# Convolution loop of a decoder step: the splitting of weight units 4 to 15 moves from GpSimd to ScalarE and VectorE

## The chip, the core and the metric

The kernel runs on one core of one Trainium2 chip. The metric is the device time of one execution in microseconds (us), and a profile of one execution shows what each engine did: TensorE (PE, with its weight loads as PEld), VectorE (DVE), ScalarE (ACT), GpSimd (POOL) and the queue of SyncE (SP), which issues loads.

## The reference

A step of a small decoder trunk: layer 0 is a Conformer convolution module with a SwiGLU feed-forward, layer 1 stick-breaking attention with another. There are 1024 prompt positions and 8 x 4 sample positions, 1056 columns in all, with 1024 channels in float32. The change lies in the first half of the convolution module:

```python
def conformer_conv(h, buf, w_pw1, b_pw1, w_dw, b_dw, ln_g, ln_b, w_pw2, b_pw2):
    a = h @ w_pw1 + b_pw1
    d = a.shape[-1] // 2
    u = a[..., :d] * jax.nn.sigmoid(a[..., d:])
    full = jnp.concatenate([buf.astype(u.dtype), u], axis=1)
    new_buf = full[:, full.shape[1] - (CONV_WIDTH - 1):]
    c = lax.conv_general_dilated(
        full, w_dw[:, None, :].astype(u.dtype), window_strides=(1,), padding='VALID',
        dimension_numbers=('NWC', 'WIO', 'NWC'), feature_group_count=d) + b_dw
    c = jax.nn.silu(layer_norm(c, ln_g, ln_b))
    return c @ w_pw2 + b_pw2, new_buf
```

`h` is the RMS-normed input, `w_pw1` is 1024 x 2048, and the depthwise convolution has 31 taps for each channel.

## The kernel before, in words

**Weights in two halves.** A product keeps float32 precision with operands of the rounded type fp32r: each weight w is split into wh, its rounding, and wl = w - wh, and each activation into xh and xl. `project` (L1255) multiplies wh by xh, wh by xl and wl by xh for each of 8 blocks of 128 input channels, so 24 matmuls of 352 columns for a tile. The weights come as a stream of units of 128 x 1024 (128 output channels, 512 KB). SP loads unit u into `w_raw` (2 slots) once unit u - 2 is split, GpSimd rounds it into `wh` (CAST, L530) and subtracts to make `wl` (TENSOR_TENSOR, L532), rings of 4 slots each. A slot may be written when the unit four before it is used up, which TensorE says with `w_done` at the first matmul of its next unit. `w_split` counts finished low halves, `w_hi` the roundings, `w_in` the loads. `unit_ready(u)` on TensorE waits until unit u has both halves.

**Chunks.** The convolution works on 8 chunks of 128 channels. Chunk c uses units 2c (linear half) and 2c+1 (gate half). On TensorE a chunk is: wait for both units; for each of three column tiles, project the linear half into a bank A and the gate half into a bank B (144 matmuls in all, L1255); then the last seven of the 31 taps as matmuls with diagonal matrices (28 matmuls, L1302; chunk 6 has 8 taps and chunk 7 has 16 there); they wait for the gated rows. Then comes the next chunk.

**ScalarE**, for chunk c (`conv_chunk`): builds the diagonals (L680) once the taps of chunk c - 1 are done, takes the sigmoid of each gate tile (L686), issues the store of u_tail, and after the taps of chunk c copies their sums with the bias into `cv` (L694), where VectorE adds the rest.

**VectorE** makes the gated rows of a chunk (`glu_rows`, L976, L982: three tiles into `ub` or, for odd chunks, into the memory of `ssq`) and then the other 24 taps (`conv`, L1000, 48 operations of 128x512, for two column halves; 46 and 30 in chunks 6 and 7). It is written one chunk behind: rows of chunk c+1, then taps of chunk c. The loop on VectorE:

```python
        glu_rows(0, 0)
        with v.Fori(0, KC // 2 - 1) as it:
            glu_rows(it, 1)
            conv(it, 0)
            glu_rows(it + 1, 0)
            conv(it, 1)
        glu_rows(KC // 2 - 1, 1)
```

**GpSimd** splits units 0 to 15 in a loop (`split_units(0, UNITS_CONV)`), then computes the convolution of the sample positions for chunks 0 to 5 and then for 6 and 7 (`decode_conv`, L558 and L561, 62 operations for each part; the first part waits for the rows of chunk 5, the second for those of chunk 7), and then goes on with units 16 and up. Behind the taps come the layer norm's mean (L1316), variance (L1324) and the second projection.

Of the kernel before, what the change touches and what calls it, by code (L numbers as in the profile page):

```python
# [20 lines left out]
F32 = mybir.dt.float32  # L21
F32R = mybir.dt.float32r
I32 = mybir.dt.int32
ALU = mybir.AluOpType
ACT = mybir.ActivationFunctionType
# [4 lines left out]
KC = D // P  # L30
# [14 lines left out]
LOOP_CHUNKS = KC - 2  # L45
# [3 lines left out]
def pe_taps(c):  # L49
    return LATE_PE_TAPS[c - LOOP_CHUNKS] if isinstance(c, int) and c >= LOOP_CHUNKS else PE_TAPS  # L50


def conv_ops_before(c):

    late = range(LOOP_CHUNKS, c) if isinstance(c, int) else ()
    return c * CONV_OPS - 2 * sum(pe_taps(i) - PE_TAPS for i in late)
SLOT = PAD + NQ
RMS_EPS, LN_EPS = 1e-6, 1e-5
RAW, RING = 2, 4
# [25 lines left out]
UNITS_CONV = U_PW2  # L85
# [68 lines left out]
def wait_alone(eng, semaphore, value):  # L154

    eng.wait_ge(semaphore, value)
    eng.sem_inc(PASSED[0], 1)
# [11 lines left out]
def build(nc, x_t, params, wstream, conv_state, cache_kt, cache_v, page_table, bias_row, bias_dec,  # L169
# [3 lines left out]
    def sem(name):  # L173
        return ctx.enter_context(nc.semaphore(name))

    def sb(name, shape, dt=F32, stack=None):
        return (stack or ctx).enter_context(nc.sbuf_tensor(name, shape, dt))
# [7 lines left out]
    w_raw = sb("w_raw", [P, RAW, KC * P])  # L185
    wh = sb("wh", [P, RING, KC * P], F32R)
    wl = sb("wl", [P, RING, KC * P], F32R)
# [71 lines left out]
    def diag(k):  # L259
        return diag_memory[k // 8][:, k % 8 * P:(k % 8 + 1) * P]  # L260
# [11 lines left out]
    def pcol(name, c):  # L272
        if isinstance(c, int):
            return par[:, off[name] + c:off[name] + c + 1]
        return par[:, ds(c + off[name], 1)]
# [4 lines left out]

    w_in = [sem(f"w_in{i}") for i in range(RAW)]
    w_hi = sem("w_hi")
    w_split = sem("w_split")
    w_done = sem("w_done")
    x_in = [sem(f"x_in{tg}") for tg in range(NTG)]
# [26 lines left out]
    class Glu:  # L312
# [6 lines left out]
        conv = sem("conv_step")  # L319
# [10 lines left out]
        act = sem("ln_act")  # L330
# [168 lines left out]
    def _(pool):  # L499
# [22 lines left out]
        def split_units(first, last):  # L522
            with pool.Fori(0, (last - first) // 4) as it:
                for s in range(4):
                    u = it * 4 + (first + s)
                    q, r = divmod(first + s, RAW)
                    pool.wait_ge(w_in[r], (it * (4 // RAW) + (q + 1)) * 16)
                    wait_alone(pool, w_done, u + 2)
                    slot = (first + s) % RING
                    pool.tensor_copy(wh[:, slot], w_raw[:, r]).then_inc(w_hi, 1)  # L530
                    pool.wait_ge(w_hi, u + 1)
                    pool.tensor_tensor(wl[:, slot], w_raw[:, r], wh[:, slot].bitcast(F32), ALU.subtract)\  # L532
                        .then_inc(w_split, 1)

        split_units(0, UNITS_CONV)


        pool.wait_ge(us_in, 16)
# [87 lines left out]
    def _(act):  # L626
# [45 lines left out]

        act.wait_ge(par_in, 16)
        act.wait_ge(n_mix0.ready, NTG * KC)
        def conv_chunk(it, u):
            c = it * 2 + u
            taps = pe_taps(c)
            wait_alone(act, Glu.taps, c + 1)
            for k in range(taps):
                mm = act.activation(diag(k), ident[:], ACT.Copy, scale=pcol("w_dw", c * W + (W - taps + k)))  # L680
            mm.then_inc(Glu.diag, 1)
            for tg in range(NTG):
                j = it * (2 * NTG) + (u * NTG + tg)
                act.wait_ge(Glu.done, j + 1)
                wait_alone(act, Glu.out, j + 3)
                act.activation(sq[:, tg % 2], B[tg][:, 0:TG], ACT.Sigmoid, bias=pcol("b_pw1", c + KC))\  # L686
                   .then_inc(Glu.sig, 1)

            wait_alone(act, Glu.out, it * (2 * NTG) + (u * NTG + 3 + NTG))
            act.dma_start(u_tail[ds(c, 1)].rearrange("a p n -> (a p) n"), ubs[u][:, SEQ:SEQ + PAD])\  # L690
               .then_inc(Glu.saved[u], 16)
            wait_alone(act, Glu.taps, c + 2)
            for h in range(2):
                ins = act.activation(cv[:, ds(c, 1), h * QT:(h + 1) * QT].rearrange("p a t -> p (a t)"), DN[h][:],  # L694
                                     ACT.Identity, bias=pcol("b_dw", c))
            ins.then_inc(Glu.init, 1)

        with act.Fori(0, LOOP_CHUNKS // 2) as it:
            conv_chunk(it, 0)
            conv_chunk(it, 1)  # L700
        conv_chunk(LOOP_CHUNKS // 2, 0)
        conv_chunk(LOOP_CHUNKS // 2, 1)
        act.dma_start(us_tail, us[:]).then_inc(Glu.dec_saved, 16)


# [213 lines left out]
    def _(v):  # L919
# [47 lines left out]
        def glu_rows(half, u):  # L967

            c = half * 2 + u
            for tg in range(NTG):  # L970
                v.wait_ge(Glu.sig, c * NTG + (tg + 1))
                if tg == 0:
                    v.wait_ge(Glu.saved[u], half * 16 + 16)
                    v.wait_ge(Glu.conv, c * CONV_OPS + CONV_OPS)
                n = TG if tg < NTG - 1 else PT2
                ins = v.scalar_tensor_tensor(out=ubs[u][:, PAD + tg * TG:PAD + tg * TG + n], in0=A[tg][:, 0:n],  # L976
                                             scalar=pcol("b_pw1", c), in1=sq[:, tg % 2, 0:n],
                                             op0=ALU.add, op1=ALU.mult)
                if tg == NTG - 1:
                    row = us[:, c, :, PAD:SLOT] if isinstance(c, int) else \  # L980
                        us[:, ds(c, 1), :, PAD:SLOT].rearrange("p a b q -> p (a b) q")
                    ins = v.scalar_tensor_tensor(  # L982
                        out=row, in0=A[tg][:, PT2:TG].rearrange("p (b q) -> p b q", q=NQ), scalar=pcol("b_pw1", c),
                        in1=sq[:, tg % 2, PT2:TG].rearrange("p (b q) -> p b q", q=NQ), op0=ALU.add, op1=ALU.mult)
                ins.then_inc(Glu.out, 1)

        def conv(half, u):

            c = half * 2 + u
            v.wait_ge(Glu.init, c + 1)  # L990
            done = conv_ops_before(c) + 2 * CONV_OPS
            for k in range(W - pe_taps(c)):
                tap = par[:, off["w_dw"] + c * W + k:off["w_dw"] + c * W + k + 1] if isinstance(c, int) else \
                    par[:, ds(c * W + (off["w_dw"] + k), 1)]
                for h in range(2):
                    out = cv[:, c, h * QT:(h + 1) * QT] if isinstance(c, int) else \
                        cv[:, ds(c, 1), h * QT:(h + 1) * QT].rearrange("p a t -> p (a t)")
                    if k:
                        v.wait_ge(Glu.conv, done + (2 * k + h - 1))
                    v.scalar_tensor_tensor(out=out, in0=ubs[u][:, h * QT + k:h * QT + k + QT], scalar=tap, in1=out,  # L1000
                                           op0=ALU.mult, op1=ALU.add).then_inc(Glu.conv, 1)


        glu_rows(0, 0)
# [3 lines that stand above are left out]
            glu_rows(it + 1, 0)  # L1008
            conv(it, 1)
        glu_rows(KC // 2 - 1, 1)  # L1010
        conv(KC // 2 - 1, 0)
        conv(KC // 2 - 1, 1)


        def ln_centre(tg):
# [632 lines left out]
```

## Time and profile before

| | |
|---|---|
| median of 3 runs | 2946.99 us (2940.54 to 2951.22) |
| profiled execution, its own time | 2943.93 us |
| its span, first to last instruction | 2941.9 us |
| busy: PE, PEld | 2753.4 us (94%), 2619.8 us (89%) |
| busy: DVE, ACT, POOL | 1295.7 us (44%), 646.2 us (22%), 1063.8 us (36%) |
| mean granted clock of TensorE | 0.962 of full speed |

Shares of the whole span say little here, since the stages differ: the projection and feed-forward stages fill TensorE, while in the convolution loop, from about 60 to 412 us, VectorE is busy most of the time. Times in the rows are microseconds from the start of the span. Operations on one engine overlap a little, so a group's time divided by its count is nearer to the spacing of two operations than the duration of one is.

### The profile page before, as it was taken

Reading aid. Unit: us, or ns where it says so; the run is one execution under the profiler, and the core shown is the slowest. Engines: PE = TensorE matmul, PEld = TensorE weight load, DVE = VectorE, ACT = ScalarE, POOL = GpSimd, SP = SyncE. Lnnn points to the kernel's source line nnn. Section 1 sums busy time; section 2 is a strip of 40 time slices with the busy share of each in tenths; the row PEclk is TensorE's granted clock in tenths of the full one; section 3 lists DMA queues with packets and bytes.
Section 4 is the critical chain, followed back from the end, with each engine's and each line's share of the span. In section 5 each row is a group of like instructions: output and inputs, shape, how many; then the busy total and the mean of one; then the engine's idle time right before and its main releaser. Section 6 shows DMA issues by size and latency. Waiting matters only on the chain.

```text
span 2941.9 us, 42757 instructions
## 1 busy us (share of the span) xinstructions
PE 2753.4 (94%) x16800; PEld 2619.8 (89%) x16800; DVE 1295.7 (44%) x2082; ACT 646.2 (22%) x1247; POOL 1063.8 (36%) x758
## 2 busy tenths in 40 slices
PE   4999859999999999998999899999889999999997
PEld 3777528899999999998989799999889999999997
DVE  6599985512222222246115488832342222222226
ACT  4111124310000000013112488821120000000002
POOL 2257962132322322223222366633332222332220
PEclk9999879999999999999999899998799999999999
DMA  3000011011111111113524443343211111111111
GB/s 127 22 22 30 8 37 37 29 58 44 44 50 44 44 50 44 43 44 107 160 78 128 133 112 102 104 140 96 99 50 51 44 44 43 44 51 51 43 44 59
DMA packets 81565, 188.27 MB, mean 64 GB/s; under 512 B 25939, under 2 KB 40659, under 8 KB 81140
## 3 DMA queue, kind: packets, MB, share of 16 engines
q1 hardware_dynamic: 58132, 149.19, 16.4%
q10 hardware_dynamic: 23264, 36.61, 4.1%
q8 instruction: 132, 2.16, 0.3%
q14 instruction: 37, 0.30, 0.0%
HBM read 154.79 MB, written 30.99 MB: 63 GB/s over the span
## 4 chain that ended last, share of the span: by engine, by line
PE 81%; DVE 10%; issue 5%; ACT 3%; ACTq 0%; DVEq 0%; DMA 0%; POOL 0%; POOLq 0%
PE bank L1255 51%; PE bank L1361 15%; PE bank L1462 5%; DVE cv L1000 3%; PE bank L1446 2%; DVE xg L945 2%; PE bank L1302 1%; PE bank L1530 1%; PE bank L1433 1%; DVE xl L949 1%; PE bank L1434 1%; DVE ssq L935 1%; PE bank L1492 1%; PE bank L1324 0%; DVE x L1229 0%
## 5 line engine op out<-in xcount | busy, mean ns | idle before, releaser
L1255 PE MATMUL bank<-xh,wh 128*128 128x352 f32 x3456 | 1139.5, 330 | 35.2 <-DVE xl L949 18.2
L1255 PE MATMUL bank<-xh,wl 128*128 128x352 f32 x3456 | 1122.6, 325 | 0.0
L1255 PE MATMUL bank<-xl,wh 128*128 128x352 f32 x3456 | 1122.4, 325 | 0.0
L530 POOL CAST wh<-w_raw 128x1024 fp32r<-128x1024 f32 x180 | 273.6, 1520 | 1537.9 <-PE bank L1255 1328.8
L1255 PEld LDWEIGHTS bank<-xh,wh 128*128 128x128 f32 x3456 | 660.0, 191 | 50.8 <-issue 18.1
L1255 PEld LDWEIGHTS bank<-xl,wh 128*128 128x128 f32 x3456 | 662.2, 192 | 2.1 <-issue 1.9
L1255 PEld LDWEIGHTS bank<-xh,wl 128*128 128x128 f32 x3456 | 660.6, 191 | 0.0
L532 POOL TENSOR_TENSOR wl<-w_raw,wh 128x1024 fp32r<-128x1024 f32 x180 | 436.4, 2424 | 14.4
L1067 DVE TENSOR_TENSOR bank<-bank,sg 128x352 f32<-128x352 f32 x132 | 70.3, 532 | 802.7 <-ACT sg L754 802.7
L1361 PE MATMUL bank<-hh,wh 128*128 128x352 f32 x1056 | 343.9, 326 | 16.4 <-DVE x L1078 13.8
L1361 PE MATMUL bank<-hl,wh 128*128 128x352 f32 x1056 | 339.4, 321 | 0.0
L1361 PE MATMUL bank<-hh,wl 128*128 128x352 f32 x1056 | 339.1, 321 | 0.0
L1078 DVE TENSOR_TENSOR x<-bank,x 128x352 f32<-128x352 f32 x480 | 249.6, 523 | 199.2 <-PE bank L1361 199.2
L754 ACT ACTIVATE sg<-bank 128x352 f32<-128x352 f32 x132 | 61.4, 465 | 1210.2 <-PE bank L1255 1210.2
L1361 PEld LDWEIGHTS bank<-hh,wh 128*128 128x128 f32 x1056 | 198.2, 188 | 24.1 <-DVE x L1078 19.7
L1361 PEld LDWEIGHTS bank<-hl,wh 128*128 128x128 f32 x1056 | 198.5, 188 | 0.2
L1361 PEld LDWEIGHTS bank<-hh,wl 128*128 128x128 f32 x1056 | 198.2, 188 | 0.0
L1462 PE MATMUL bank<-at_sb,v_sb 128*128 128x128 f32 x1152 | 157.2, 280 | 0.4 <-DVE at_sb L1163 0.4
L1462 PEld LDWEIGHTS bank<-at_sb,v_sb 128*128 128x128 f32 x1152 | 142.7, 192 | 5.5 <-DVE at_sb L1163 0.6
L1000 DVE SCALAR_TENSOR_TENSOR cv<-ssq,par,cv 128x512 f32 (+1 forms) x174 | 139.7, 880 | 0.0
L1000 DVE SCALAR_TENSOR_TENSOR cv<-ub,par,cv 128x512 f32 (+1 forms) x190 | 136.4, 794 | 0.0
L641 ACT ACTIVATE sq<-x 128x352 f32<-128x352 f32 x120 | 59.5, 498 | 286.4 <-DVE x L1216 143.2
(147 smaller groups left out, 2530.6 us busy)
## 6 DMA issues: line engine op xcount, KB each, us to landing
w_raw<-wstream SPq DMA_DIRECT2D x196, 512.0 KB, 3.5
k_sb<-k_split SPq DMA_DIRECT2D x16, 512.0 KB, 3.5
kp<-cache_kt SPq DMA_DIRECT2D x16, 512.0 KB, 4.1
vp<-cache_v SPq DMA_DIRECT2D x16, 512.0 KB, 5.1
x<-x_t ACTq DMA_DIRECT2D x3, 1408.0 KB, 12.0
k_t<-stage ACTq DMA_DIRECT2D x8, 528.0 KB, 2.8
y_t<-x ACTq DMA_DIRECT2D x24, 176.0 KB, 2.0
k_split<-stage_h ACTq DMA_DIRECT2D x16, 256.0 KB, 4.6
```

The costliest lines, as they stand in the source:

```text
L530: pool.tensor_copy(wh[:, slot], w_raw[:, r]).then_inc(w_hi, 1)
L532: pool.tensor_tensor(wl[:, slot], w_raw[:, r], wh[:, slot].bitcast(F32), ALU.subtract)\
L641: act.activation(sq[:, j % 2], tile, ACT.Square).then_inc(n.sq, 1)
L754: act.activation(sg[:, jj % 2], A[jj % 3][:, 0:TG], ACT.Silu).then_inc(f.silu, 1)
L945: v.scalar_tensor_tensor(out=xg[:, j % 3], in0=x[:, c, tgs(tg)], scalar=pcol(g_name, c), in1=rstd[:, tgs(tg)], op0=ALU.mult, op1=ALU.mult) ...
L1000: v.scalar_tensor_tensor(out=out, in0=ubs[u][:, h * QT + k:h * QT + k + QT], scalar=tap, in1=out, op0=ALU.mult, op1=ALU.add).then_inc(Glu. ...
L1067: v.tensor_tensor(hidden, hidden, sg[:, jj % 2], ALU.mult).then_inc(f.mul, 1)
L1078: v.tensor_tensor(x[:, c, tgs(tg)], DN[n % 2][:, 0:TG], x[:, c, tgs(tg)], ALU.add)\
L1255: mm = pe.matmul(out, a[:, slot, w], b[:, k, tgs(tg)], start=(k == 0 and i == 0), stop=(k == KC - 1 and i == 2))
L1361: mm = pe.matmul(DN[n % 2][:, 0:TG], a[:, s + c // 4, w], b[:, 2 * parity + kk, tgs(tg)], start=first, stop=(kk == 1 and i == 2))
L1446: mm = pe.transpose(TB[g % 2][:, cols], s_sb[:, g % NZ, cols], ident[:])
L1462: mm = pe.matmul(out, v_sb[:, seg.low + b, DH * e:DH * e + P], at_sb[:, g % AT_TILES, seg.off + b * P:seg.off + (b + 1) * P], start=(g % P ...
```

## The change

GpSimd splits units 0 to 3 alone. In the loop of ScalarE each of chunks 0 to 5 rounds two units, 2c+4 and 2c+5: the first behind the store of u_tail, the second behind the start values of the chunk. VectorE makes their low halves in `conv` of the same chunk, behind taps 6 and 14 of its 24, so behind 14 and behind 30 of the 48 operations. The roundings are counted in a new semaphore, and GpSimd adds the twelve to `w_hi`, for its own later counts.

```diff
+    w_hi_conv = sem("w_hi_conv")
...
-        split_units(0, UNITS_CONV)
+        split_units(0, RING)
+        pool.sem_inc(w_hi, UNITS_CONV - RING)
...
-        def conv_chunk(it, u):
+        def split_hi(it, u, i):
+            unit, slot = it * 4 + (2 * u + 4 + i), 2 * u + i
+            wait_alone(act, w_in[i], (it * 2 + (u + 3)) * 16)
+            wait_alone(act, w_done, unit + 2)
+            act.activation(wh[:, slot], w_raw[:, i], ACT.Copy).then_inc(w_hi_conv, 1)
+
+        def conv_chunk(it, u, split=True):
...
             act.dma_start(u_tail[ds(c, 1)].rearrange("a p n -> (a p) n"), ubs[u][:, SEQ:SEQ + PAD])\
                .then_inc(Glu.saved[u], 16)
+            if split:
+                split_hi(it, u, 0)
             wait_alone(act, Glu.taps, c + 2)
             for h in range(2):
                 ins = act.activation(cv[:, ds(c, 1), h * QT:(h + 1) * QT].rearrange("p a t -> p (a t)"), DN[h][:],
                                      ACT.Identity, bias=pcol("b_dw", c))
             ins.then_inc(Glu.init, 1)
+            if split:
+                split_hi(it, u, 1)
...
-        def conv(half, u):
+        def split_lo(half, u, i):
+            unit, slot = half * 4 + (2 * u + 4 + i), 2 * u + i
+            v.wait_ge(w_hi_conv, unit - (RING - 1))
+            v.tensor_tensor(wl[:, slot], w_raw[:, i], wh[:, slot].bitcast(F32), ALU.subtract).then_inc(w_split, 1)
+
+        def conv(half, u, split=True):
...
                     v.scalar_tensor_tensor(out=out, in0=ubs[u][:, h * QT + k:h * QT + k + QT], scalar=tap, in1=out,
                                            op0=ALU.mult, op1=ALU.add).then_inc(Glu.conv, 1)
+                if split and k in (6, 14):
+                    split_lo(half, u, k // 14)
```

Chunks 6 and 7 are called with `split=False` on both engines.

How the instructions stand now. First VectorE in the loop, chunk 0 of an iteration (the taps read `ub`), from tap 14 on: the second low half, which `w_split` counts, stands behind 30 of the chunk's tap operations.

```order
L1020 SCALAR_TENSOR_TENSOR cv<-ub,par,cv 128x512
L1019 REGISTER_ALU
L1020 SCALAR_TENSOR_TENSOR cv<-ub,par,cv 128x512 [waits conv_step]
L1004 REGISTER_ALU
L1005 TENSOR_TENSOR wl<-w_raw,wh 128x1024 [waits w_hi_conv]
L1019 REGISTER_ALU
L1020 ISA [waits conv_step]
L1020 SCALAR_TENSOR_TENSOR cv<-ub,par,cv 128x512
```

Before, the same place had taps alone, and no instruction of VectorE was counted by `w_split`.

```order
L1000 SCALAR_TENSOR_TENSOR cv<-ub,par,cv 128x512
L999 REGISTER_ALU
L1000 SCALAR_TENSOR_TENSOR cv<-ub,par,cv 128x512 [waits conv_step]
L999 REGISTER_ALU
L1000 ISA [waits conv_step]
L1000 SCALAR_TENSOR_TENSOR cv<-ub,par,cv 128x512
```

Then TensorE from the taps of chunk 0 to the projection of chunk 1, after the change, with bank numbers. It is the same in the kernel before: all matmuls of a projection stand behind one wait on `w_split` for both units of the chunk.

```order
L1324 MATMUL bank6<-ub,xg 128x512 [waits glu_out,conv_diag]
L1324 MATMUL bank6<-ub,xg 128x512 x6
L1324 MATMUL bank7<-ub,xg 128x512 x7
L1277 MATMUL bank0<-xh,wh 128x352 [waits glu_out,w_split]
L1277 MATMUL bank0<-xl,wh 128x352
```

Last ScalarE between the last sigmoid of a chunk and the first diagonal of the next, before:

```order
L690 DMA u_tail<-ub 128x30
L156 REGISTER_ALU
L694 ISA [waits conv_taps]
L694 ACTIVATE cv<-bank,par 128x512
L694 ISA
L694 ACTIVATE cv<-bank,par 128x512
L680 ISA [waits conv_taps]
L680 ACTIVATE xg<-ident,par 128x128
```

and after:

```order
L700 DMA u_tail<-ub 128x30
L156 ISA
L156 ISA [waits w_in0]
L683 ACTIVATE wh<-w_raw 128x1024 [waits w_done]
L156 REGISTER_ALU
L706 ISA [waits conv_taps]
L706 ACTIVATE cv<-bank,par 128x512
L706 ISA
L706 ACTIVATE cv<-bank,par 128x512
L156 REGISTER_ALU [waits w_in1]
L683 ACTIVATE wh<-w_raw 128x1024 [waits w_done]
L690 ISA [waits conv_taps]
```

Both roundings stand in ScalarE's order, the second one, with its waits for a load and for TensorE, ahead of the diagonals of the next chunk.

## Rows read from the trace of the kernel before

**Rows 1.** Timeline of VectorE: start us, us, engine line op out<-in xcount.

```profile
109.64 34.81 DVE L1000 SCALAR_TENSOR_TENSOR cv<-ub,par,cv 128x512 f32 x48
...
187.77 31.88 DVE L1000 SCALAR_TENSOR_TENSOR cv<-ub,par,cv 128x512 f32 x48
...
224.61 33.53 DVE L1000 SCALAR_TENSOR_TENSOR cv<-ssq,par,cv 128x512 f32 x48
...
261.52 34.71 DVE L1000 SCALAR_TENSOR_TENSOR cv<-ub,par,cv 128x512 f32 x48
...
299.58 46.60 DVE L1000 SCALAR_TENSOR_TENSOR cv<-ssq,par,cv 128x512 f32 x48
...
349.50 35.01 DVE L1000 SCALAR_TENSOR_TENSOR cv<-ub,par,cv 128x512 f32<-128x512 f32 x46
```

**Rows 2.** Chain of waits, in order of time: start us, us, what.

```profile
148.07 15.12 PE bank L1302 x28
163.19 23.18 PE bank L1255 x144
188.00 12.26 PE bank L1302 x28
200.26 22.95 PE bank L1255 x144
```

**Rows 3.** Timeline of TensorE, taps: in brackets the idle time before, and its releaser.

```profile
148.07 14.26 PE L1302 MATMUL bank<-ub,xg 128*128 128x512 f32 x26 [3.00 <-DVE us L982]
...
224.84 12.26 PE L1302 MATMUL bank<-ub,xg 128*128 128x512 f32 x28 [1.65 <-DVE us L982]
...
349.74 2.05 PE L1302 MATMUL bank<-ssq,xg 128*128 128x512 f32 x2 [11.32 <-DVE us L982]
```

**Rows 4.** Timeline of GpSimd in the loop, units 9 and 10, then 15.

```profile
163.52 17.10 POOL L530 CAST wh<-w_raw 128x1024 fp32r<-128x1024 f32 x1 [15.74 <-PE bank L1255]
180.70 2.41 POOL L532 TENSOR_TENSOR wl<-w_raw,wh 128x1024 fp32r<-128x1024 f32 x1
183.05 1.04 POOL L530 CAST wh<-w_raw 128x1024 fp32r<-128x1024 f32 x1
...
274.34 22.80 POOL L530 CAST wh<-w_raw 128x1024 fp32r<-128x1024 f32 x1 [9.13 <-PE bank L1255]
```

**Rows 5.** VectorE's taps from 199 to 240 us: duration ns min/median/max.

```profile
L1000 DVE SCALAR_TENSOR_TENSOR cv<-ssq,par,cv x21: 737/737/2381, 224.6 to 239.5; 128x512 f32 x21
```

**Rows 6.** Groups from 160 to 500 us: line engine op shapes xcount | busy us, mean ns.

```profile
L1030 DVE TENSOR_TENSOR xl<-xg,xh 128x352 fp32r<-128x352 f32 x24 | 12.6, 525 | 8.6 <-ACT xh L729 7.3
...
L976 DVE SCALAR_TENSOR_TENSOR ub<-bank,par,sq 128x352 f32<-128x352 f32 x4 | 2.3, 584 | 1.7 <-ACT sq L686 1.4 <-DVE cv L1000 0.3
...
L729 ACT ACTIVATE xh<-xg 128x352 fp32r<-128x352 f32 x24 | 11.9, 498 | 0.8
```

**Rows 7.** Timeline of ScalarE in the loop.

```profile
163.43 1.27 ACT L694 ACTIVATE cv<-bank,par 128x512 f32 x2 [16.25 <-PE bank L1302]
164.59 2.16 ACT L680 ACTIVATE xg<-ident,par 128x128 f32<-128x128 f32 x7
...
201.79 1.28 ACT L680 ACT_TABLE_LOAD   x1
```

**Rows 8.** Windows: stretch us, PE, PEld, DVE, ACT, POOL busy, granted clock, DMA, GB/s.

```profile
341.00:349.70 8.70, 0.00 (x0) 0.00 (x0) 7.16 (x11) 1.11 (x2) 8.31 (x12) 0.53 0.00 0
349.70:355.00 5.30, 5.26 (x7) 2.20 (x8) 5.30 (x6) 0.00 (x0) 5.06 (x7) 0.50 0.03 6
...
477.80:485.00 7.20, 7.11 (x34) 7.11 (x35) 5.77 (x13) 3.47 (x7) 0.00 (x0) 0.74 0.00 0
```

**Rows 9.** Timeline of GpSimd, first decode operation of either part.

```profile
299.52 0.52 POOL L558 TENSOR_TENSOR q_dec<-us,par 128x192 f32<-128x192 f32 x1
...
356.77 0.74 POOL L558 TENSOR_TENSOR q_dec<-us,par 128x64 f32<-128x64 f32 x1
```

**Rows 10.** Loads of weights: KB each, median us to landing.

```profile
w_raw<-wstream SPq DMA_DIRECT2D x196, 512.0 KB, 3.5
```

More of the change, by code:

```diff
@@ L700, in _ @@
             conv_chunk(it, 1)
-        conv_chunk(LOOP_CHUNKS // 2, 0)
-        conv_chunk(LOOP_CHUNKS // 2, 1)
+        conv_chunk(LOOP_CHUNKS // 2, 0, split=False)
+        conv_chunk(LOOP_CHUNKS // 2, 1, split=False)
         act.dma_start(us_tail, us[:]).then_inc(Glu.dec_saved, 16)
@@ L1010, in _ @@
         glu_rows(KC // 2 - 1, 1)
-        conv(KC // 2 - 1, 0)
-        conv(KC // 2 - 1, 1)
+        conv(KC // 2 - 1, 0, split=False)
+        conv(KC // 2 - 1, 1, split=False)
         def ln_centre(tg):
```

## The prediction

> **What bounds the kernel now.** I read the timeline of VectorE through the convolution loop first, then the chain of waits, then the timelines of TensorE and GpSimd. I call the parts of chunk c proj(c) (144 matmuls on units 2c and 2c+1), glu(c), taps(c) (28 matmuls of the seven last taps) and conv(c) (48 tap operations on VectorE). The VectorE rows show the order glu(c+1), conv(c), glu(c+2), conv(c+1): conv(0) starts at 109.64, conv(2) at 187.77, conv(3) at 224.61, conv(4) at 261.52, conv(5) at 299.58 and conv(6) at 349.50 [rows 1]. From 187.77 to 261.52 a chunk takes 36.9 us. Two rings are nearly in balance there. TensorE needs 12.26 us for taps and 22.95 to 23.18 for a projection [rows 2], with 1.65 us idle between them while the last tile of glu is made [rows 3]: 36.9. VectorE needs 31.88 us for 48 taps that nothing disturbs [rows 1], start to start (31.88 - 0.74) / 47 = 0.663 us, and some 3.3 for glu: 35.2. So VectorE has 1.7 us to spare per chunk, unless GpSimd gets in its way.
>
> GpSimd splits the weights and is never what is waited for. Its rounding (CAST) of a unit that begins beside running taps takes 17.10 to 22.80 us, against 1.04 in a gap, and its subtraction 2.41 [rows 4]. Unit 9's low half ends at 180.70 + 2.41 = 183.1, and proj(4), which needs units 8 and 9, starts after taps(3), at 200.26 [rows 2, 4]: 17 us early. In return a GpSimd subtraction holds up a tap: one takes 2.38 us where the median is 0.74 [rows 5]. All such excess over 0.663 per tap is 34.81 - 31.88 = 2.93 us in conv(0), 33.53 - 31.88 = 1.65 in conv(3) and 34.71 - 31.88 = 2.83 in conv(4) [rows 1]: **7.4 us**, all that freeing GpSimd can give back to VectorE.
>
> **The change, step by step.** *Removed:* 12 roundings and 12 subtractions on GpSimd, units 4 to 15. They lie on no path but for the 7.4 us.
>
> *Added on ScalarE:* 12 roundings of 128x1024. A copy of 128x352 takes 0.498 us [rows 6], three of them 1.5, and 1024 elements are fewer than three times 352: at most 1.5 us. ScalarE has time: it waits up to 16.25 us at a stretch for taps [rows 7]. The first rounding of chunk c stands behind the store of u_tail and ahead of the start values of conv(c); it waits for the load of unit 2c+4, issued behind the low half of 2c+2 at conv(c-1) + 10.4, so until about conv(c-1) + 15. taps(c) end at 12.5, and the start values queued behind it are needed only after glu(c+1), at 49: hidden. The second stands behind those start values and waits for the first matmul of proj(c+1).
>
> *Added on VectorE:* 12 subtractions of 128x1024. No row has this shape. The same operation on 128x352 takes 0.525 us [rows 6], and a longer operation costs (0.737 - 0.584) / 160 = 0.96 ns per element more (tap of 512 against glu of 352) [rows 5, 6]: 0.525 + 672 x 0.96 ns = 1.17, say 1.2 us, and 1.15 as spacing. Bounds: half of it, 0.6, and GpSimd's own 2.4 [rows 4]. Two per chunk are 2.3 us.
>
> *What moves is the decisive thing.* The low half of unit 2c+5 now comes after 30 of the 48 taps of conv(c), and proj(c+2) starts with both units 2c+4 and 2c+5. But conv(c) itself starts only after glu(c+1), just as taps(c+1) start on TensorE, and taps last 12.26 us. So at conv(c) + 12.5 TensorE is ready for proj(c+2), and the second low half is there at 30 x 0.663 + 1.15 + 1.2 = 22.2. **TensorE waits 9.8 us in each of six chunks**, for proj(2) to proj(7). Nothing gives it back: conv(c+1) must wait for glu(c+2), and so for proj(c+2). A chunk then takes 22.2 + 0.1 (handing over) + 23.1 (projection) + 1.4 (last glu tile: 163.19 + 23.18 = 186.37, conv at 187.77 [rows 1, 2]) = 46.8 us.
>
> *The clock.* A wait of 9.8 us is new for TensorE in this loop. Behind 11.32 us of idle ahead of 349.74 [rows 3] the granted clock is 0.50 until 355, so 1.2 GHz where full speed is 2.4 [rows 8]: 5.3 us at half clock, 2.7 lost. Taps take 15.12 us behind 3.00 us of idle, against 12.26 behind 1.65 [rows 2, 3], so 2.9 lost; the stretch from 477.8 has 0.74 over 7.2 us [rows 8], 1.9 lost. I take 2.7, the row with the nearest idle stretch; bounds 0 and 2.9. The Trainium skill, TensorE: Matmul & The Clock Gate, section Why this matters for your kernels, asks for matmul bursts without idle between them, since idling brings the half clock back. It speaks against this change; by it the six waits cost more than their length, and the rows say the same. A chunk is then **49.5 us**.
>
> *The decode convolution on GpSimd* waits for glu(5) but now starts only at 299.52, being queued behind unit 15 [rows 9]. After the change it starts with conv(4). While it runs, a tap takes 46.60 / 48 = 0.97 us instead of 0.663 [rows 1]. In conv(4) the 30 taps ahead of the second low half become 29.1 and each subtraction perhaps 0.3 longer: 9.8 us more, once. In exchange its first part (192 columns, 62 operations, from 299.52 to 356.8 [rows 9]) is over before conv(5), which saves its share of conv(6): (356.8 - 349.5) us at 0.3 in 0.97, 2.3 us. The second part still starts with conv(6).
>
> *Sum.* conv(0) still starts near 109.6. Six steps from there to conv(6): 6 x 49.5 + 9.8 = 306.8 us, against 349.50 - 109.64 = 239.9 before: +66.9. Less 2.3 at the end of the taps: **+64.6**. Loads are no term: the one for unit 2c+6 is issued behind the low half of 2c+4 and lands 3.5 us later [rows 10], ahead of need. Behind the loop nothing changes but that GpSimd's splits of units 16 on and the mean matmuls shift along. The profiled execution was 2943.93 us, so 3008.5; the median of the runs shown is 3.1 above it, so **3012**.
>
> **Rivals.**
> (a) *The wait without the clock.* The projection gets its full clock at once, as taps do behind 1.65 us of idle [rows 3]. Against it are the three stretches above [rows 2, 3, 8]. 6 x 2.7 less: +48.4, **2995 us**. Between it and the forecast lies the 1.9 of 477.8: 3007.
> (b) *The wait is longer, through ScalarE.* ScalarE stands in order: its second rounding waits for a load that is issued only as proj(c+1) starts, then come seven diagonals and the first sigmoid of glu(c+1). Load 3.5, rounding 1.5, diagonals 2.16 and two table loads of 1.28 [rows 7, 10] make 9.7 us, against 23.1 / 3 = 7.7 until the first tile of the projection is done at full clock and some 10 with the loss. The last tile is done only at 23: a load would have to take some 10 us more to make it late. With 3 us per chunk: +18, **3030 us**. A subtraction of 2.4 us on VectorE gives about as much (12 x 1.2 = 14, 3026).
> (c) *No wait: the low half is in time.* This needs it by conv(c) + 12.5, so the second subtraction at tap 7 or earlier instead of 14. If the weights were in time all the same, say because taps(c+1) is held up as long, the loop would be bound by VectorE, 35.2 + 2.3 = 37.5 us a chunk. Against before that is -0.7 for conv(0) (2.3 more, 2.93 less), +0.6 each for conv(2) and conv(3), and for conv(4), beside which the decode convolution now runs, 48 x 0.97 + 2.9 + 3.3 = 52.8 for 38.1: +14.7. conv(5) has the rest of that first part, 37.5 + 3 for 49.9: -9.4, and the end -2.3. In all +3.5, **2950 us**, no change. The semaphore counts of the diff exclude it, as far as I can read them.
> (d) *The relief of VectorE decides.* This would be the 7.4 us, with all subtractions hidden in VectorE's idle time: 2940 us, just inside 0.3%; I count it as faster all the same. By the Trainium skill, GPSIMD Engine Reference, section Performance versus the Vector engine, a two-input operation is done in half the time on VectorE; engine by engine the move looks right, and the rule alone would forecast this case. No row has the shape on VectorE. It would need (c) as well.
>
> **How the numbers follow.** Forecast 0.75, (a) 0.10, (b) 0.12, (c) 0.02, (d) 0.01. The likeliest time is 3012. The range takes in (a) with a subtraction somewhat shorter, and (b): 2990 to 3032. Under 0.3% (8.8 us) a measurement of this kernel can't tell from no change. Faster 0.01, same 0.02, slower 0.97.
>
> **What would show it.** In the profile after, the first matmul of a projection should wait for VectorE's wl, some 9.8 us each, six times (some 19 for proj(6)); the starts of conv should stand 49 to 50 us apart, and the one from conv(4) to conv(5) 59; VectorE should idle about 12 us in a chunk, before the last glu tile; no tap over 0.75 us before conv(4), the granted clock at half as each of these projections begins; GpSimd's decode operations should start with conv(4), at about 109.6 + 4 x 49.5 = 308 us. If projections start right behind the taps, the forecast is wrong at its root; if they wait but the clock stays full, only its second term is.

## The result and the profile after

The changed kernel takes 3010.07 us (median of 6 runs, 3004.48 to 3017.71), the kernel before 2948.36 us beside it: 61.7 us more, a ratio of 1.0213 with a 95% interval of 1.02 to 1.0225. The forecast was 3012 us, 64.6 us more than before. The profiled execution took 3008.92 us with a span of 3006.5 us.

The groups of the page that answer to the change: line, engine, operation, count | busy us, mean ns | idle time before, with what ended most of it.

```profile
L1277 PE MATMUL bank<-xh,wh 128*128 128x352 f32 x3456 | 1143.1, 331 | 102.4 <-DVE wl L1005 66.7
...
L531 POOL CAST wh<-w_raw 128x1024 fp32r<-128x1024 f32 x168 | 178.3, 1061 | 1409.0 <-PE bank L1277 1199.7
...
L533 POOL TENSOR_TENSOR wl<-w_raw,wh 128x1024 fp32r<-128x1024 f32 x168 | 407.3, 2424 | 13.4
```

The first line is the result in short: the projections now wait 66.7 us in all for VectorE's low halves (`wl`, L1005), a releaser that the kernel before did not have. These are six waits. The timeline of TensorE shows each, the first matmul of proj(2), then of proj(6) and proj(7):

```profile
131.34 0.63 PE L1277 MATMUL bank<-xh,wh 128*128 128x352 f32 x1 [9.84 <-DVE wl L1005]
...
336.70 0.64 PE L1277 MATMUL bank<-xh,wh 128*128 128x352 f32 x1 [19.25 <-DVE wl L1005]
...
385.55 0.63 PE L1277 MATMUL bank<-xh,wh 128*128 128x352 f32 x1 [8.13 <-DVE wl L1005]
```

Those of proj(3), proj(4) and proj(5) are 9.84 us too. VectorE's timeline from the taps of chunk 0 on, the counterpart of [rows 1], shows where the low half stands:

```profile
109.01 9.35 DVE L1020 SCALAR_TENSOR_TENSOR cv<-ub,par,cv 128x512 f32 x14
118.29 1.22 DVE L1005 TENSOR_TENSOR wl<-w_raw,wh 128x1024 fp32r<-128x1024 f32 x1
119.42 10.68 DVE L1020 SCALAR_TENSOR_TENSOR cv<-ub,par,cv 128x512 f32 x16
130.02 1.22 DVE L1005 TENSOR_TENSOR wl<-w_raw,wh 128x1024 fp32r<-128x1024 f32 x1
131.16 12.02 DVE L1020 SCALAR_TENSOR_TENSOR cv<-ub,par,cv 128x512 f32 x18
143.73 0.58 DVE L990 SCALAR_TENSOR_TENSOR ub<-bank,par,sq 128x352 f32<-128x352 f32 x1 [0.56 <-ACT sq L696]
149.70 0.58 DVE L990 SCALAR_TENSOR_TENSOR ub<-bank,par,sq 128x352 f32<-128x352 f32 x1 [5.38 <-ACT sq L696]
157.32 0.55 DVE L990 SCALAR_TENSOR_TENSOR ub<-bank,par,sq 128x320 f32<-128x320 f32 x1 [7.04 <-ACT sq L696]
157.78 0.24 DVE L996 SCALAR_TENSOR_TENSOR us<-bank,par,sq 128x32 f32 x1
157.94 9.36 DVE L1020 SCALAR_TENSOR_TENSOR cv<-ssq,par,cv 128x512 f32 x14
```

The second low half ends at 130.02 + 1.22 = 131.24, and proj(2) starts at 131.34. The bill comes after 143.2: VectorE is out of taps and idles 0.56 + 5.38 + 7.04 = 13.0 us while proj(2) runs. Each engine waits once for the other in every chunk. The projections in the chain of waits stand against 22.95 to 23.18 of [rows 2]:

```profile
131.34 25.20 PE bank L1277 x144
...
180.28 24.65 PE bank L1277 x144
...
228.65 26.18 PE bank L1277 x144
...
278.56 25.00 PE bank L1277 x144
...
336.70 25.17 PE bank L1277 x144
...
385.55 24.42 PE bank L1277 x144
```

Their mean is 25.10. The granted clock is in the windows of the changed kernel: the wait, the first 4.7 us of proj(2), the rest of it (columns as in [rows 8]).

```profile
121.60:131.30 9.70, 0.00 (x0) 0.00 (x0) 9.70 (x15) 2.21 (x3) 0.00 (x0) 0.70 0.11 46
131.30:136.00 4.70, 4.66 (x17) 4.69 (x18) 4.70 (x8) 0.82 (x1) 0.00 (x0) 0.53 0.31 112
136.00:156.50 20.50, 20.50 (x129) 20.24 (x128) 8.35 (x13) 6.08 (x12) 0.00 (x0) 1.00 0.00 1
```

The steps from one conv to the next, from VectorE's timelines:

| | conv(0) to (1) | (1) to (2) | (2) to (3) | (3) to (4) | (4) to (5) | (5) to (6) | sum | taps of 6 and 7 |
|---|---|---|---|---|---|---|---|---|
| before | 38.20 | 39.93 | 36.84 | 36.91 | 38.06 | 49.92 | 239.9 | 62.7 |
| forecast | 49.5 | 49.5 | 49.5 | 49.5 | 59.3 | 49.5 | 306.8 | 60.4 |
| after | 48.93 | 48.38 | 49.91 | 48.73 | 58.25 | 48.10 | 302.3 | 62.3 |

So the loop is 62.4 us longer, conv(0) starts 0.6 us earlier and the taps end at 473.6 instead of 412.2, 61.4 us later. That is the change in the medians. The two profiled executions differ by 65.0; the other 3.6 us lie behind the convolution, and no step of the change accounts for them. That of the kernel before was 4.4 us under its median and that of the changed kernel 1.2 us, so 3.3 us of the 65.0 come from which executions were profiled.

### The profile page after: what moved, and what is told of

Read it like the earlier page. It is cut to its first block, busy times and chain, and to the rows that moved or that the text cites. A ratio compares the mean times of both kernels' runs of the same rounds, so it can differ in the third digit from the quotient of the medians.

```text
span 3006.5 us, 42757 instructions
## 1 busy us (share of the span) xinstructions
PE 2761.2 (92%) x16800; PEld 2630.5 (87%) x16800; DVE 1303.3 (43%) x2094; ACT 657.8 (22%) x1259; POOL 938.5 (31%) x734
## 4 chain that ended last, share of the span: by engine, by line
PE 82%; DVE 10%; issue 5%; ACT 3%; ACTq 0%; DVEq 0%; DMA 0%; POOL 0%
PE bank L1277 53%; PE bank L1383 15%; PE bank L1484 4%; DVE cv L1020 3%; PE bank L1468 2%; DVE xg L959 1%; DVE xl L963 1%; PE bank L1552 1%; PE bank L1455 1%; PE bank L1456 1%; DVE ssq L949 1%; PE bank L1514 1%; PE bank L1324 0%; PE bank L1346 0%; DVE x L1251 0%
## 5 line engine op out<-in xcount | busy, mean ns | idle before, releaser
L1277 PE MATMUL bank<-xh,wh 128*128 128x352 f32 x3456 | 1143.1, 331 | 102.4 <-DVE wl L1005 66.7
L531 POOL CAST wh<-w_raw 128x1024 fp32r<-128x1024 f32 x168 | 178.3, 1061 | 1409.0 <-PE bank L1277 1199.7
L533 POOL TENSOR_TENSOR wl<-w_raw,wh 128x1024 fp32r<-128x1024 f32 x168 | 407.3, 2424 | 13.4
L560 POOL TENSOR_TENSOR q_dec<-us,par 128x192 f32<-128x192 f32 (+1 forms) x62 | 51.1, 824 | 314.9 <-DVE us L996 314.9
L1020 DVE SCALAR_TENSOR_TENSOR cv<-ub,par,cv 128x512 f32 (+1 forms) x190 | 143.3, 829 | 0.0
L1020 DVE SCALAR_TENSOR_TENSOR cv<-ssq,par,cv 128x512 f32 (+1 forms) x174 | 125.6, 801 | 0.0
```

The costliest lines, as they stand in the source:

```text
L560: pool.tensor_tensor(tap, us[:, chunks, :, k:k + NQ], per_chunk(w_all[:, chunks, k]), ALU.mult)\
L1277: mm = pe.matmul(out, a[:, slot, w], b[:, k, tgs(tg)], start=(k == 0 and i == 0), stop=(k == KC - 1 and i == 2))
```

## The experiments

Each edit is against the changed kernel unless said otherwise. Theory W says that TensorE waits for the second low half because of where it stands among the taps. Theory V puts the loss on VectorE's added load and the early decode convolution.

**The place of the subtractions: e1, e2, e3.**

```diff
-                if split and k in (6, 14):
-                    split_lo(half, u, k // 14)
+                if split and k in (2, 6):
+                    split_lo(half, u, k // 6)
```

> The changed kernel, but the two subtractions of a chunk stand behind taps 2 and 6 instead of 6 and 14, so the second is done at conv(c) + 14 x 0.663 + 2.35 = 11.6 us, before TensorE has finished taps(c+1) at 12.5. Theory W (TensorE waits for the second low half): the wait of 9.8 us and the clock's loss go in all six chunks, VectorE's 37.5 us per chunk bounds the loop, and the time is that of case (c), 2950 us; steps of conv 37 to 38 us. Theory V (the loss is VectorE's added 14 us and the early decode convolution, whatever their place): nothing changes, 3010 us.

e2 has (6, 10) there:

> The changed kernel with the second subtraction behind tap 10 instead of 14: 8 tap operations earlier, 5.3 us in five chunks and 7.8 in the one beside the decode convolution. Theory W: the wait is 4.5 us instead of 9.8, each step of conv some 43.5 us, 34 us less in all: 2976 us. Theory V: 3010 us.

e3 has (6, 18):

> The changed kernel with the second subtraction behind tap 18 instead of 14: 8 tap operations later. Theory W: the wait is 15.1 us, each step of conv some 54 us, 34 us more in all: 3044 us. Theory V: 3010 us.

| second subtraction behind tap | expected | median us | runs | ratio to before (95%) | steps of conv(0) to conv(3) |
|---|---|---|---|---|---|
| 6 (e1) | 2950 | 2954.26 | 11 | 1.0013 (1.0003 to 1.0022) | 37.6, 38.8, 37.6, 37.6 |
| 10 (e2) | 2976 | 2979.96 | 2 | 1.0104 (1.0083 to 1.0125) | 43.0, 43.9, 43.9, 44.1 |
| 14 (the change) | | 3010.07 | 6 | 1.0213 (1.02 to 1.0225) | 48.9, 48.4, 49.9, 48.7 |
| 18 (e3) | 3044 | 3050.80 | 2 | 1.0344 (1.0323 to 1.0365) | 54.8, 54.9, 54.6, 54.6 |

The same instructions at four places give four times. From 6 to 10, 14 and 18 the time rises by 26, 30 and 41 us; each move puts eight tap operations, 5.3 us, ahead of the low half. TensorE's waits for it, in total, number and longest, are these in e2 and in e3, against 66.7 us in the changed kernel:

```profile
PE bank L1277 <- DVE wl L1005: 33.0, 6, 11.5
...
PE bank L1277 <- DVE wl L1005: 100.9, 6, 27.0
```

They move by 34 us each way; the medians, of two runs each, move by 30 and 41. Theory V, which gives 3010 for all, is out. With the subtractions at 2 and 6 the waits are nearly gone. What the waits of e1 show for VectorE's low halves, from 60 to 500 us (total, times, longest):

```profile
PEld bank L1277 <- DVE wl L1005: 5.3, 4, 4.6
...
PE bank L1277 <- DVE wl L1005: 3.8, 1, 3.8
```

One wait of 3.8 us is left. The steps of 37.56 us are VectorE's own, forecast at 37.5. e1 is 0.13% slower than the kernel before: that is VectorE's added load, less what the freed GpSimd gives back.

**The clock: e4 and e9.** TensorE gets matmuls to fill its waits; their results are overwritten unused.

```diff
             mm.then_inc(Glu.taps, 1)
+            for _ in range({1: 21, 2: 21, 3: 21, 4: 21, 5: 42, 6: 17}.get(it * 2 + u, 0)):
+                pe.matmul(A[0][:], mean_w[:], x[:, 0, 0:QT], start=True, stop=True)
```

> The changed kernel, and TensorE fills each of the six waits with matmuls whose results are not used (21 of 512 columns, some 9.2 us; 42 ahead of proj(6), 17 ahead of proj(7)). The weights arrive as late as before, so theory W alone leaves 3010 us. If the half clock behind the wait costs what the projections of the changed kernel show (25.1 us against 23.1), the six projections go back to 23.1 us each: 12 us less, 2998 us. If the matmuls outlast the wait, up to 3 us of that are lost again.

It took 3053.36 us (4 runs), 43 more than the changed kernel: my size was wrong. One such matmul is two records of the trace, as the timeline of e9 shows (20 records for 10 matmuls) and the count of e4 (286 records for 143), so the filling lasted 18.2 us and outlasted the wait. e9 has 10, 10, 10, 10, 20 and 8:

```profile
121.42 8.75 PE L1327 MATMUL bank<-x,mean_w 128*128 128x512 f32 x20
131.43 0.40 PE L1277 MATMUL bank<-xh,wh 128*128 128x352 f32 x1 [1.26 <-DVE wl L1005]
```

> The fill again, sized by what its first form showed (a float32 matmul of 512 columns is two records of 0.44 us, so 0.87 us each): 10 in four waits, 20 ahead of proj(6), 8 ahead of proj(7), 8.8, 17.5 and 7.0 us. The weights arrive as late as in the changed kernel, but TensorE is busy until about 1 us before. If the half clock costs what the projections show, they take 23.1 us instead of 25.1 and the time falls by 12 us: 2998 us, steps of conv 47 us. If the clock has no part in it: 3010 us.

e9: 3002.34 us (5 runs), ratio 1.0182 (1.0165 to 1.02) against 1.0213 (1.02 to 1.0225) of the change, 7.7 us less, between the 12 and the nothing that were expected. The chain of waits of e9 has the projections back at full speed:

```profile
131.43 23.14 PE bank L1277 x144
...
178.31 23.42 PE bank L1277 x144
```

All six are 23.14 or 23.42 (mean 23.28), and the granted clock over the first is 1.00:

```profile
131.60:155.00 23.40, 22.96 (x144) 22.67 (x143) 12.83 (x20) 7.12 (x13) 0.00 (x0) 1.00 0.07 23
```

The steps fall to 46.89, 47.15, 47.16, 46.89, 56.29 and 47.27 us, 291.7 against 302.3. The weights arrive as late as in the changed kernel: proj(2) starts 22.33 us after conv(0) in both. In the profiled executions 10.6 us of the 62.4 come back, in the medians 7.7. That share of the loss is the clock's.

**The subtractions among the gated rows: e5.**

```diff
+        def glu_rows(half, u, split=True):
...
                 ins.then_inc(Glu.out, 1)
+                if split and tg < 2:
+                    slot = 2 * (1 - u) + tg
+                    v.wait_ge(w_hi_conv, half * 4 + (2 * u - 1 + tg))
+                    v.tensor_tensor(wl[:, slot], w_raw[:, tg], wh[:, slot].bitcast(F32), ALU.subtract)\
+                     .then_inc(w_split, 1)
...
-                if split and k in (6, 14):
-                    split_lo(half, u, k // 14)
```

The rows of chunks 0 and 7 are called with `split=False`.

> The changed kernel, but the subtractions for units 2c+4 and 2c+5 stand among the gated rows of chunk c+1, behind the first and the second tile, where VectorE waits some 0.7 us for ScalarE's next sigmoid. Theory W: low halves are ready before taps(c+1) begin, TensorE never waits. Each subtraction of 1.15 us hides 0.7 of itself, VectorE needs 35.2 + 0.9 = 36.1 us per chunk, less than TensorE's 36.9, so the loop is bound by TensorE as before and GpSimd's 7.4 us are gained in part: 2945 us, 0 to 5 us under the kernel before. Theory V: 3010 us. If the loop's steps stay over 37.5 us, the place among the rows costs as much as among the taps: 2950 us.

2948.43 us (12 runs), ratio 0.9991 (0.9979 to 1.0004), so no gain that can be told from zero. The first steps are 36.86, 37.08, 36.85 and 37.09 us, TensorE's pace. Timeline of VectorE, rows of chunk 3:

```profile
177.94 0.58 DVE L990 SCALAR_TENSOR_TENSOR ssq<-bank,par,sq 128x352 f32<-128x352 f32 x1 [0.15 <-DVE cv L1025]
178.44 1.21 DVE L1003 TENSOR_TENSOR wl<-w_raw,wh 128x1024 fp32r<-128x1024 f32 x1
179.57 0.58 DVE L990 SCALAR_TENSOR_TENSOR ssq<-bank,par,sq 128x352 f32<-128x352 f32 x1
180.07 1.21 DVE L1003 TENSOR_TENSOR wl<-w_raw,wh 128x1024 fp32r<-128x1024 f32 x1
182.36 0.55 DVE L990 SCALAR_TENSOR_TENSOR ssq<-bank,par,sq 128x320 f32<-128x320 f32 x1 [1.08 <-ACT sq L696]
```

The subtractions fill the gaps of some 0.7 us in which VectorE waited for a sigmoid, and VectorE still waits 1.08 us for the last tile. Later the gain is spent: conv(4) and conv(5) take 50.4 and 41.5 us, 91.9 together, where the kernel before has 88.0, since the decode convolution starts a chunk earlier.

**GpSimd subtracts, ScalarE rounds: e6.**

```diff
-                if split and k in (6, 14):
-                    split_lo(half, u, k // 14)
...
         pool.sem_inc(w_hi, UNITS_CONV - RING)
+        for n in range(RING, UNITS_CONV):
+            pool.wait_ge(w_hi_conv, n - (RING - 1))
+            pool.tensor_tensor(wl[:, n % RING], w_raw[:, n % RAW], wh[:, n % RING].bitcast(F32), ALU.subtract)\
+                .then_inc(w_split, 1)
```

> The changed kernel, but GpSimd makes the low halves of units 4 to 15 again, from ScalarE's roundings; VectorE has none. Low halves are early, TensorE never waits. If GpSimd's subtraction holds up VectorE as in the kernel before (1.6 to 2.1 us each, twelve of them, against the 7.4 us of before) the loop takes up to 14 us more than before in VectorE-bound chunks: 2950 to 2958 us. If it waits for a gap like the roundings did, 2943 us.

2954.94 us (12 runs), ratio 1.0018 (1.0005 to 1.0031). GpSimd's timeline shows two kinds:

```profile
124.07 5.31 POOL L540 TENSOR_TENSOR wl<-w_raw,wh 128x1024 fp32r<-128x1024 f32 x1 [10.10 <-ACT wh L687]
...
150.72 2.77 POOL L540 TENSOR_TENSOR wl<-w_raw,wh 128x1024 fp32r<-128x1024 f32 x1 [21.34 <-ACT wh L687]
165.84 18.95 POOL L540 TENSOR_TENSOR wl<-w_raw,wh 128x1024 fp32r<-128x1024 f32 x1 [12.35 <-ACT wh L687]
189.81 2.77 POOL L540 TENSOR_TENSOR wl<-w_raw,wh 128x1024 fp32r<-128x1024 f32 x1 [5.02 <-ACT wh L687]
202.68 21.19 POOL L540 TENSOR_TENSOR wl<-w_raw,wh 128x1024 fp32r<-128x1024 f32 x1 [10.10 <-ACT wh L687]
```

A subtraction that arrives some 2 us after conv begins runs at once and holds up one tap (the longest is 2.84 us). Of those that arrive in the middle of the taps, four wait about 20 us for the end of conv, but the one at 124.07, in conv(0), is done after 5.31 us and holds up a tap of 2.89 us; why, no run shows. The time lies in the first of the two ranges that were expected, 2950 to 2958, with some subtractions behaving by the one case and some by the other.

**The price of the subtractions: e7**, against e1:

```diff
-            v.tensor_tensor(wl[:, slot], w_raw[:, i], wh[:, slot].bitcast(F32), ALU.subtract).then_inc(w_split, 1)
+            v.sem_inc(w_split, 1)
```

> As the kernel with subtractions behind taps 2 and 6, but without them: the low halves of units 4 to 15 are left out (the memory keeps those of units 0 to 3) and only counted. This prices VectorE's 12 subtractions once TensorE doesn't wait. If VectorE bounds the loop then, they cost 37.5 - 36.9 = 0.6 us in balanced chunks and 2.3 to 3 in the later ones: 6 to 10 us less than the kernel with them. If they are hidden, no difference.

2945.51 us (10 runs), 8.8 less than e1, in the middle of what was expected; ratio 0.9979 (0.9965 to 0.9992). The steps fall from 37.56 to 36.85. Twelve subtractions of 1.14 us are 13.7 us of VectorE, so some 5 hide by the medians; in the profiled executions the taps end 6.9 us sooner after conv(0), and some 7 hide.

**The decode convolution: e8.**

```diff
+        pool.wait_ge(Glu.out, 3 + NTG * 7)
         pool.wait_ge(us_in, 16)
```

> The changed kernel, with the decode convolution held until the rows of chunk 6, so that its first part runs beside conv(5) as in the kernel before. Theory W: the wait ahead of proj(6) falls from some 19 to 9.8 us and that ahead of proj(7) rises by the same, the sum stays: 3010 us, within 3. If the early start were a loss of its own (theory V), the time falls by some 10 us.

3010.73 us (2 runs). The steps (4) to (5) and (5) to (6) are 48.40 and 57.70 instead of 58.25 and 48.10: the longer step has moved by one chunk and the sum, 106.1 against 106.35, has not. In the changed kernel the early start is no loss of its own.

**GpSimd rounds, VectorE subtracts: e10**, against e1. Without ScalarE's two roundings per chunk:

```diff
-            if split:
-                split_hi(it, u, 0)
...
-            if split:
-                split_hi(it, u, 1)
...
         pool.sem_inc(w_hi, UNITS_CONV - RING)
+        for n in range(RING, UNITS_CONV):
+            pool.wait_ge(w_in[n % RAW], (n // RAW + 1) * 16)
+            pool.wait_ge(w_done, n + 2)
+            pool.tensor_copy(wh[:, n % RING], w_raw[:, n % RAW]).then_inc(w_hi_conv, 1)
```

> VectorE subtracts behind taps 2 and 6 as in e1, but GpSimd rounds units 4 to 15 as before the change, and ScalarE none. If ScalarE's part of the change matters little, the loop takes what e1 takes, 2954 us; a rounding that arrives beside running taps waits some 20 us for a gap, as before the change, but is there before conv(c) needs it. If it came too late for the subtraction behind tap 2, VectorE would wait in each chunk: up to 10 us a chunk, 3010 us. In e1 ScalarE's second rounding waits for a load and delays nothing that counts; if it did, this kernel is faster than e1.

2963.22 us (6 runs), ratio 1.0051 (1.0034 to 1.0068), slower than e1, which I had not expected. No rounding waits 20 us there. GpSimd in chunk 1, whose taps start at 147.74:

```profile
156.59 3.68 POOL L541 CAST wh<-w_raw 128x1024 fp32r<-128x1024 f32 x1 [31.33 <-DMA w_raw<-wstream]
163.03 1.33 POOL L541 CAST wh<-w_raw 128x1024 fp32r<-128x1024 f32 x1 [2.77 <-DMA w_raw<-wstream]
```

The first rounding ends 0.9 us behind VectorE's second subtraction, which runs from 158.15 to 159.37. The second runs almost at once, in the middle of the taps. The last 34 taps of the chunk take 24.18 us where e1 has 22.61, and each of the first four steps is 39.1 instead of e1's 37.56 to 38.78. Rounding on ScalarE is worth 1.5 us in such a chunk. From conv(0) to the end of the taps the profiled executions differ by 5.5 us; the medians differ by 9.0, and the rest has no explanation here.

**A version that is faster than both: e11**, e5 and e8 together.

> The kernel with the subtractions among the gated rows (e5), and the decode convolution held until the rows of chunk 6 as in e8. Its first part then runs beside conv(5), whose step is longer than 36.9 us anyway through TensorE's eighth tap, instead of beside conv(4) and part of conv(5). The two steps should take 36.9 + 50.4 us instead of 50.4 + 41.5, and the taps of chunks 6 and 7 0.5 us more: 4 us less than e5, 2944 us, 5 us or 0.2% under the kernel before. If GpSimd's work costs the same wherever it stands, no difference from e5, 2948 us.

2943.73 us (12 runs) against 2949.59 of before beside it: ratio 0.9978 (0.9967 to 0.999). The timeline of VectorE from conv(4) to the end of the taps:

```profile
257.39 31.89 DVE L1026 SCALAR_TENSOR_TENSOR cv<-ub,par,cv 128x512 f32 x48
...
294.19 46.25 DVE L1026 SCALAR_TENSOR_TENSOR cv<-ssq,par,cv 128x512 f32 x48
...
343.79 35.27 DVE L1026 SCALAR_TENSOR_TENSOR cv<-ub,par,cv 128x512 f32<-128x512 f32 x46
378.99 27.01 DVE L1026 SCALAR_TENSOR_TENSOR cv<-ssq,par,cv 128x512 f32<-128x512 f32 x30
```

The steps (4) to (5) and (5) to (6) are 36.8 and 49.6, 86.4 instead of e5's 91.9. Taps that nothing disturbs (31.89) stand up to conv(4), and the taps end at 406.0 where the kernel before has 412.2. The gain of 5.9 us is 0.2%, small, but the interval leaves out 1.

## Why the prediction was right, step by step

- *What moves.* Right: four waits of 9.84 us forecast at 9.8, and 19.25 ahead of proj(6) forecast at some 19. Only the one ahead of proj(7) is shorter, 8.13, since chunk 6 has an eighth tap on TensorE, some 1.75 us (12.26 us for seven taps [rows 3]) that the forecast left out. That the wait is the cause is shown by e1, e2 and e3.
- *The subtraction on VectorE.* 1.22 us, forecast at 1.2 from the shape of 352 by a slope of two other rows; spacing 1.13 to 1.14 where no decode operation runs. The rounding on ScalarE takes 1.06, bounded by 1.5. It hides, as forecast: ScalarE waits 15.10 and 9.52 us for loads in chunk 1, and no sigmoid of a last tile is late. Rival (b) didn't occur.
- *The clock.* Right in kind and too large in size: the projections took 25.10 against my 23.1, 2.0 us each instead of 2.7, so 12 instead of 16.2. e9 shows it from the other side, 10.6 us in its profile and 7.7 in the medians. I had taken the row with the nearest idle stretch; 1.9, the only row in which a projection and not the taps followed the wait, was the better one. Rival (a), without the clock, is out.
- *The decode convolution.* Its first part starts at 305.19, with conv(4), and that step is 9.4 us longer than the mean of the other five, forecast at 9.8. The 2.3 us at the end did not come: 62.3 against 62.7. The taps of chunk 6 are shorter, 32.91 against 35.01 [rows 1], but those of chunk 7 take 29.45 instead of 27.73, since GpSimd's splits of units 16 to 18 now lie wholly beside them, where before they began at 401.66, with 10.5 us of taps left:

```profile
444.14 29.45 DVE L1020 SCALAR_TENSOR_TENSOR cv<-ssq,par,cv 128x512 f32<-128x512 f32 x30
```

```profile
456.38 1.58 POOL L531 CAST wh<-w_raw 128x1024 fp32r<-128x1024 f32 x1
458.04 2.67 POOL L533 TENSOR_TENSOR wl<-w_raw,wh 128x1024 fp32r<-128x1024 f32 x1
```

  I had these splits only "shift along". This is the step that failed, by 2 us, and it offsets half of the error on the clock. So it is partly luck that the total, 61.7 us against 64.6, is as near as it is.
- *What goes.* No tap before conv(4) takes over 0.752 us, so the 7.4 us are gone as said. They are worth nothing while TensorE's wait sets the pace. With the wait away (e5, e11) part of them shows.
- *Rivals (c) and (d).* (c) gave 2950 for a kernel without the wait; e1 is that kernel, 2954.26. Its steps are 37.56, 38.78, 37.56, 37.56, 52.58 and 40.77 against my 37.5, 39.9, 37.5, 37.5, 52.8 and 40.5. (d), moved to VectorE with all of it hidden, comes nearest in e5 and was worth 1.2 us, not told from zero; only with the decode convolution put back in its place is there a gain.

The Trainium skill, GPSIMD Engine Reference, section Performance versus the Vector engine, has a two-input operation done in half the time on VectorE. The trace agrees: 1.22 us against 2.42. Yet this gain per operation was nothing beside 9.84 us of waiting.

## What to carry to other kernels

Before work moves onto a busy in-order engine, lay its new place in time beside the moment its consumer is ready: here 30 taps ahead of a low half cost 62 us, while the twelve operations themselves, 1.2 us each, cost 7 to 9 us where they make nobody wait (e7), and eight tap operations earlier or later are 26 to 41 us. Where the producer's phase begins only together with the consumer's last short phase, here 12.3 us of taps, a step has no longer than that to be in time. And when an engine is freed, look at what it does next: its next job may start sooner, beside something that it slows down.

## What the runs showed of the hardware

- A GpSimd operation on 1024 columns that arrives while VectorE's taps run back to back often waits until they end (18.95 and 21.19 us in e6, 17.10 to 22.80 in [rows 4]), its subtraction as well as its rounding. But not always: e6's subtraction at 124.07 took 5.31 us, e10's second rounding 1.33, and the kernel before has one in conv(0), which the prediction's 17.10 to 22.80 leaves out:

```profile
122.47 4.06 POOL L530 CAST wh<-w_raw 128x1024 fp32r<-128x1024 f32 x1 [14.22 <-PE bank L1255]
```

  When GpSimd gets in, it is VectorE that is held up: one tap by about 2.1 us for a subtraction of e6. In the decode convolution, where one GpSimd operation follows another, both go on, and each tap takes 0.97 us. The Trainium skill, SBUF — State Buffer, section SBUF: two separate sides, says that the pair of ports which VectorE and GpSimd share is locked for a whole instruction, the other one blocked. The held-up tap agrees with it. A wait through some thirty taps, each an instruction of its own, is more than it says, and what decides whether GpSimd gets in between taps was not tried.
- Behind a wait of 9.84 us the granted clock was 0.53 over the first 4.7 us of the projection; behind a wait filled with matmuls up to 1.26 us before, it was 1.00 (e9).
- A float32 matmul of 512 columns takes 0.87 us at the full clock here, in two records of 0.44 (e9: 20 records in 8.75 us).
